# A decoder trunk on one Trainium2 core: the softmax probabilities of all four heads are multiplied by one over their sum on ScalarE, none on VectorE

## The chip, the core and the metric

The kernel runs on one core of a Trainium2 chip. The core has a matrix engine (TensorE, PE in the profile, with its weight loads as PEld), a vector engine (VectorE, DVE), a scalar engine (ScalarE, ACT), a general engine (GpSimd, POOL) and a queue that issues transfers (SyncE, SP). Each engine takes its instructions in the order in which they were written, and they meet through counting semaphores: an instruction adds one when it is done, and others wait for a count. The metric is the time of one execution on the device in microseconds, the median of several runs.

## The reference, cut to what matters

Two layers of a decoder on 1024 tokens with 1024 channels in float32. Layer 0 mixes with a retention, layer 1 with a sliding-window attention; behind each comes an MLP with a squared ReLU. The change lies in the attention of layer 1:

```
scores = q k^T * dh**-0.5            # 128 queries against 256 keys: the block before and its own
scores = where(mask, scores, -inf)
probs  = softmax([scores, sink])     # the sink, one number per head, only adds to the sum
o      = probs[..., :-1] v
```

There are 16 query heads in 4 groups that share a key and a value head each, so a group has 4 query heads. The 1024 tokens are 8 blocks of 128 queries. One block of one group is therefore a matrix of 128 queries (the partitions) by 4 heads by 256 keys, each head of which is to be divided by its own sum in each row.

## The kernel before, in words

Products of float32 are made as three products of a high and a low part: ACT rounds an operand to its high part, DVE subtracts to get the low part, and PE runs hi x hi, hi x lo and lo x hi (`product`, L480 to L482). Layer 0 comes first, the attention of layer 1 runs from about 1565 to 2000 us, and the MLP of layer 1 follows.

The attention is a pipeline over 32 items, i = 8 g + t, for group g of 0 to 3 and block t of 0 to 7. The function `sw_steps` writes, for each engine, one step s at a time, and in a step the parts of several items side by side. Group 0 is written out, groups 1 and 2 are a hardware loop of two turns, group 3 is written out and has two steps more, in which the pipeline drains and the next stage begins. In step s the engines do, in this order:

- PE: `a_pe`, the projection of block s to queries, keys and values (24 matmuls); `b_pe`, the transposes of queries and keys of block s-1 (L1797 to L1799); `d_pe`, the eight transposes of the probabilities of block s-2 (L1816), which wait for the semaphore sw_prob; half of `f_pe`, the output projection of earlier blocks; `c_pe`, the scores of block s-1; the other half of `f_pe`; `e_pe`, probabilities times values of block s-2.
- ACT: `sq_act`, squares for the norm of block s (L1856); `qkT_act`, qT_hi and kT_hi of block s-1 (L1881, L1882); `copy_act` (L1863, L1866); `pT_act`, the high part of the transposed probabilities of block s-2; now and then a split of weights; `exp_act`, four exponentials of block s-1, each with its row sum (L1897); `oT_act` (L1907); `prob_act`, the multiply of block s-1 by rden (L1873).
- DVE: `qkT_dve`, qT_lo and kT_lo of block s-1 (L1914, L1915); then the low part of v, the norm, the low part of the transposed probabilities, the mask and the maximum of block s-1, woven together; sometimes weight splits; the adds of the output projection into xT (L652); `oT_dve` (L2035); `den_dve`, the sum with the sink and its reciprocal rden (L1963); `prob_dve`, the multiply of block s-1 (L2029).
- POOL: the rotary embedding of block s (L2005 to L2023).

The probabilities lie in one buffer, prob, which the profile names xn, since it is the memory of the tile xn. It holds the masked scores, then the exponentials, then the probabilities, all in place. `prob_act` multiplies heads 2 and 3 in two instructions with one scale per row each, and only the second adds to sw_prob; `prob_dve` multiplies heads 0 and 1 in one instruction and adds one. Two increments an item are what `d_pe` waits for. Both multiplies wait for rden, through the semaphore sw_den. `den_dve` also waits until the item before has been multiplied, since rden is overwritten.

Of the kernel before, what the change touches and what calls it, by code (L numbers as in the profile page):

```python
# [25 lines left out]
ALU = mybir.AluOpType  # L26
ACT = mybir.ActivationFunctionType
AX = mybir.AxisListType

P = 128  # L30
# [3 lines left out]
TT = S // P  # L34
# [86 lines left out]
def wait(eng, sem, value):  # L121

    if isinstance(value, int) and value <= 0:
        return
    eng.wait_ge(sem, value)


def trunk(nc, x_in, positions, norm_mix, norm_mlp, w_up, w_down, ret_in, ret_out, sw_in, q_gain,
          k_gain, sinks, sw_out, c_ident, c_causal, c_mask, c_head, c_freq, c_freq_row, out, y_dram, x_dram, a_dram, r_dram):
    ctx = ExitStack()  # L130
    with ctx:
# [276 lines left out]
        sw_den = sem("sw_den")  # L408
# [1400 lines left out]

        def d_pe(pe, g, t):  # L1810
            i = TT * g + t
            pe.wait_ge(sw_prob, 2 * (i + 1))
            for s in range(2):
                wait(pe, sw_plo, 2 * (i - 1) + s + 1)
                for hh in range(4):
                    last = pe.transpose(ps[:, SP_ + s, hh * P:(hh + 1) * P], prob[:, hh, s, :], ident[:])  # L1816
                last.then_inc(d_mm, 1)
# [51 lines left out]
        def prob_act(act, g, t):  # L1869
            i = TT * g + t  # L1870
            act.wait_ge(sw_den, 2 * (i + 1))
            for hh in (2, 3):
                last = act.activation(prob[:, hh, :, :], prob[:, hh, :, :], ACT.Copy, scale=rden[:, hh:hh + 1])  # L1873
            last.then_inc(sw_prob, 1)

        def qkT_act(act, g, t):
            i = TT * g + t
# [79 lines left out]
        def den_dve(dve, g, t):  # L1957
            i = TT * g + t
            dve.wait_ge(sw_exp, 5 * (i + 1))
            wait(dve, sw_prob, 2 * i)  # L1960
            dve.tensor_tensor(den[:], ssum[:], esink[:], ALU.add).then_inc(sw_den, 1)
            dve.wait_ge(sw_den, 2 * i + 1)
            dve.reciprocal(rden[:], den[:]).then_inc(sw_den, 1)  # L1963
# [33 lines left out]
        def rope_sw_pool(pool, g, t):  # L1997
# [23 lines left out]
            pool.tensor_tensor(q4[:, :, 1, :], q4[:, :, 1, :], s4[:, 0:nq, 0, :], ALU.add)  # L2021
            pool.tensor_tensor(k3[:, 0, :], k3[:, 0, :], s4[:, nq, 1, :], ALU.subtract)
            pool.tensor_tensor(k3[:, 1, :], k3[:, 1, :], s4[:, nq, 0, :], ALU.add).then_inc(sw_radd, 1)  # L2023

        def prob_dve(dve, g, t):
            i = TT * g + t
            dve.wait_ge(sw_den, 2 * (i + 1))
            half = prob[:, 0:2, :, :].rearrange("p h s n -> p h (s n)")
            dve.tensor_tensor(half, half, rden[:, 0:2].unsqueeze(2).to_broadcast([P, 2, 2 * P]),  # L2029
                               ALU.mult).then_inc(sw_prob, 1)  # L2030

        def oT_dve(dve, g, t):
            i = TT * g + t
# [78 lines left out]
        def sw_steps(which, eng):  # L2112
# [9 lines left out]
            def run(f, g, s, lag):  # L2122
                it = item(g, s, lag)
                if it and (s - lag < TT):
                    f(eng, *it)

            def step(g, s, last_group):
# [49 lines left out]
                if which == "dve":  # L2177
                    run(qkT_dve, g, s, 1)
                    run(vlo_dve, g, s, 0)
                    run(var_dve, g, s, 0)  # L2180
                    behind = item(g, s, 2)
                    lows = [lambda j=j: pT_dve(eng, *behind, j) for j in range(2)] if behind and s - 2 < TT else []
                    softmax = item(g, s, 1)
                    masks = ([lambda j=j: mask_half(eng, *softmax, j) for j in range(2)] +
                             [lambda j=j: max_dve(eng, *softmax, j) for j in range(2)] +
                             [lambda j=j: sink_dve(eng, *softmax, j) for j in range(2)]
                             if softmax and s - 1 < TT else [])
                    if s == TT - 1 and not last_group:
                        splits = [lambda j=j: sw_split_lo(eng, g + 1, j) for j in range(4)]
                        work = lows + splits[:2] + masks[:2] + splits[2:] + masks[2:]  # L2190
                    else:
                        work = lows + masks
                    if s < TT:
                        scale_dve(eng, g, s, work)
                    else:
                        for w in work:
                            w()
                    if s in (4, 6):
                        for j in range(s, s + 2):
                            sw_split_lo(eng, g, j)  # L2200
                    behind_out = item(g, s, FLAG)
                    if last_group and s >= FLAG:
                        for m in range(4 * (s - FLAG), min(4 * (s - FLAG) + 4, KT)):
                            add(eng, DG_SW + g, m, BDS)
                        between_dve(eng, s)
                    elif behind_out:
                        for c in range(2):
                            add(eng, DG_SW + behind_out[0], 2 * behind_out[1] + c, BDS)
                    run(oT_dve, g, s, 2)
                    run(den_dve, g, s, 1)  # L2210
                    run(prob_dve, g, s, 1)
                    if begins and s == 0:
                        for m in range(KT, TILES):
                            norm_low(eng, m)
                    if begins and s == 1:
                        norm_rstd(eng, 2, 1)
                    if last_group:
                        drain_dve(eng, s)
# [332 lines left out]
```

## Time and profile before

| | us |
|---|---|
| median of 3 runs | 2682.6 |
| lowest and highest | 2678.55, 2683.26 |
| the profiled execution, whole | 2680.5 |
| its span in the profile | 2678.9 |

| engine | busy us | share of the span |
|---|---|---|
| PE | 2578.7 | 96% |
| PEld | 2153.6 | 80% |
| DVE | 1795.0 | 67% |
| ACT | 931.0 | 35% |
| POOL | 289.1 | 11% |

The times of the trace are microseconds from the start of the span. "Busy" is the time in which an engine executes; waiting is not in it. A line of the timeline gives the start, the time taken, the engine, the line of the kernel, the operation with its output and inputs, and how many instructions stand in the row; in brackets stands how long the engine had been idle before it, and which instruction ended that. Instructions of one engine overlap at their ends, so their distance from start to start is shorter than the time of one. "issue" is idle time for which the profile shows no wait.

### The profile page before, as it was taken

Reading aid. Unit: us, or ns where it says so; the run is one execution under the profiler, and the core shown is the slowest. Engines: PE = TensorE matmul, PEld = TensorE weight load, DVE = VectorE, ACT = ScalarE, POOL = GpSimd, SP = SyncE. Lnnn points to the kernel's source line nnn. Section 1 sums busy time; section 2 is a strip of 40 time slices with the busy share of each in tenths; the row PEclk is TensorE's granted clock in tenths of the full one; section 3 lists DMA queues with packets and bytes.
Section 4 is the critical chain, followed back from the end, with each engine's and each line's share of the span. In section 5 each row is a group of like instructions: output and inputs, shape, how many; then the busy total and the mean of one; then the engine's idle time right before and its main releaser. Section 6 shows DMA issues by size and latency. Waiting matters only on the chain.

```text
span 2678.9 us, 36897 instructions
## 1 busy us (share of the span) xinstructions
PE 2578.7 (96%) x11929; PEld 2153.6 (80%) x11929; DVE 1795.0 (67%) x3397; ACT 931.0 (35%) x1732; POOL 289.1 (11%) x344
## 2 busy tenths in 40 slices
PE   8999999999999999999999988999888999999999
PEld 6878878878788888888888877888767888888887
DVE  7545444454576876667677788888867666676775
ACT  6232332323311544442121255555554444311111
POOL 2102011020000300000000043322320000000000
PEclk9999999999999999999999999999989999999999
DMA  6012110121333333254222201001013323522222
GB/s 207 24 52 67 52 61 23 48 72 32 134 108 96 111 134 123 88 176 131 100 94 95 87 21 40 17 24 40 18 69 119 116 96 110 204 96 101 94 94 86
DMA packets 161735, 231.77 MB, mean 87 GB/s; under 512 B 21681, under 2 KB 103889, under 8 KB 161618
## 3 DMA queue, kind: packets, MB, share of 16 engines
q1 hardware_dynamic: 159314, 226.10, 25.8%
q10 hardware_dynamic: 2304, 4.20, 0.4%
q8 instruction: 63, 1.03, 0.2%
q14 instruction: 54, 0.44, 0.1%
HBM read 171.53 MB, written 58.73 MB: 86 GB/s over the span
## 4 chain that ended last, share of the span: by engine, by line
PE 81%; DVE 10%; issue 5%; ACT 3%; DMA 0%; POOL 0%; DVEq 0%; ACTq 0%; SPq 0%
PE ps L480 26%; PE ps L482 26%; PE ps L481 26%; ACT xn L1897 1%; DVE xT L652 1%; DVE wqg_lo L449 1%; PE ps L1292 1%; PE ps L1293 1%; DVE hT_lo L527 1%; PE ps L1294 1%; DVE smax L1944 1%; DVE pT_lo L1921 1%; DVE hss L1977 1%; PE ps L1340 0%; PE ps L1324 0%
## 5 line engine op out<-in xcount | busy, mean ns | idle before, releaser
L652 DVE TENSOR_TENSOR xT<-ps,xT 128x512 f32<-128x512 f32 x704 | 482.2, 689 | 268.1 <-PE ps L482 267.9
L480 PE MATMUL ps<-aT_hi,wd_hi 128*128 128x512 f32 x1408 | 554.9, 394 | 12.1 <-DVE xT L652 9.8
L481 PE MATMUL ps<-aT_lo,wd_hi 128*128 128x512 f32 x1408 | 550.4, 391 | 0.0
L482 PE MATMUL ps<-aT_hi,wd_lo 128*128 128x512 f32 x1408 | 550.4, 391 | 0.0
L480 PE MATMUL ps<-bh,uw_hi 128*128 128x512 f32 x880 | 343.8, 391 | 9.5 <-DVE uw_lo L740 8.6
L482 PE MATMUL ps<-bh,uw_lo 128*128 128x512 f32 x880 | 343.4, 390 | 0.0
L481 PE MATMUL ps<-bl,uw_hi 128*128 128x512 f32 x880 | 343.3, 390 | 0.0
L480 PEld LDWEIGHTS ps<-aT_hi,wd_hi 128*128 128x128 f32 x1408 | 265.9, 189 | 68.7 <-issue 13.2
L482 PEld LDWEIGHTS ps<-aT_hi,wd_lo 128*128 128x128 f32 x1408 | 265.7, 189 | 55.5
L481 PEld LDWEIGHTS ps<-aT_lo,wd_hi 128*128 128x128 f32 x1408 | 266.1, 189 | 54.2
L442 ACT ACTIVATE aT_hi<-raw 128x1024 fp32r<-128x1024 f32 x80 | 80.5, 1051 | 596.7 <-PE ps L482 583.1
L480 PEld LDWEIGHTS ps<-bh,uw_hi 128*128 128x128 f32 x880 | 165.7, 188 | 44.8 <-DVE uw_lo L740 9.2
L482 PEld LDWEIGHTS ps<-bh,uw_lo 128*128 128x128 f32 x880 | 165.8, 188 | 34.8
L481 PEld LDWEIGHTS ps<-bl,uw_hi 128*128 128x128 f32 x880 | 165.8, 188 | 34.0
L1557 DVE BATCH_NORM_STATS2 bn<-ps 128x6 f32<-128x512 f32 x32 | 22.4, 699 | 157.0 <-PE ps L482 157.0
L1897 ACT ACTIVATE xn<-xn,nmax 128x256 f32<-128x256 f32 x128 | 63.6, 498 | 145.3 <-DVE sdif L1955 145.3
L758 DVE TENSOR_TENSOR uw_lo<-raw,uw_hi 128x512 fp32r<-128x512 f32 x112 | 76.9, 690 | 53.2 <-ACT uw_hi L753 52.4
L758 DVE TENSOR_TENSOR uw_lo<-us,uw_hi 128x512 fp32r<-128x512 f32 x84 | 58.0, 692 | 74.6 <-ACT uw_hi L753 74.6
L480 PE MATMUL ps<-wqg_hi,hT_hi 128*128 128x512 f32 x256 | 100.1, 391 | 4.9 <-DVE wqg_lo L449 4.9
L480 PE MATMUL ps<-wv_hi,hT_hi 128*128 128x512 f32 x256 | 102.1, 399 | 0.0
L480 PE MATMUL ps<-ws_hi,hT_hi 128*128 128x384 f32 x256 | 89.0, 348 | 11.7 <-DVE ws_lo L1769 6.7
L482 PE MATMUL ps<-wv_hi,hT_lo 128*128 128x512 f32 x256 | 99.8, 390 | 0.0
(285 smaller groups left out, 4706.3 us busy)
## 6 DMA issues: line engine op xcount, KB each, us to landing
raw<-in_w_up SPq DMA_DIRECT2D x64, 512.0 KB, 5.5
raw<-in_w_down SPq DMA_DIRECT2D x64, 512.0 KB, 3.4
raw<-a_dram SPq DMA_DIRECT2D x64, 512.0 KB, 3.3
raw<-in_ret_w_in SPq DMA_DIRECT2D x48, 512.0 KB, 4.9
a_dram<-upost SPq DMA_DIRECT2D x64, 256.0 KB, 2.1
a_dram<-xn SPq DMA_DIRECT2D x64, 256.0 KB, 2.0
xT<-x_dram SPq DMA_DIRECT2D x24, 512.0 KB, 6.3
y_dram<-xn SPq DMA_DIRECT2D x32, 256.0 KB, 2.3
```

The source lines that it names most:

```text
L442: act.activation(dst, src, ACT.Copy).then_inc(w_hi, 1)
L449: dve.tensor_tensor(dst, src, hi.bitcast(F32), ALU.subtract).then_inc(w_lo, 1)
L480: pe.matmul(bank, ah, bh, start=(begin and i == 0), stop=False, skip_group_check=not begin)
L481: pe.matmul(bank, ah, bl, start=False, stop=False, skip_group_check=not begin)
L482: last = pe.matmul(bank, al, bh, start=False, stop=(i == len(pairs) - 1), skip_group_check=not begin)
L527: dve.scalar_tensor_tensor(hT_lo[:, k, cols], xT[:, k, cols], gain(2, k), hT_hi[:, k, cols].bitcast(F32), ALU.mult, ALU.subtract).then_inc ...
L652: dve.tensor_tensor(xT[:, k, cols], ps[:, banks[m % len(banks)], :], xT[:, k, cols], ALU.add).then_inc(x_add, 1)
L758: dve.tensor_tensor(uw(uw_lo, s % URING), weight(i, q), uw(uw_hi, s % URING).bitcast(F32), ALU.subtract).then_inc(u_lo, 1)
L1292: pe.matmul(bank, wh, hT_hi[:, k, cols], start=(k == 0), stop=False)
L1293: pe.matmul(bank, wh, hT_lo[:, k, cols], start=False, stop=False)
L1294: last = pe.matmul(bank, wl, hT_hi[:, k, cols], start=False, stop=(k == KT - 1))
L1897: act.activation(prob[:, hh, :, :], prob[:, hh, :, :], ACT.Exp, bias=nmax[:, hh:hh + 1], accum_out=ssum[:, hh:hh + 1]).then_inc(sw_exp, 1)
```

## The change

All four heads are multiplied by ACT, each in an instruction of 128 x 256 elements with its own increment of sw_prob. DVE's multiply of 128 x 512 elements is gone. The count that `d_pe` and `den_dve` wait for is four an item instead of two. Nothing else is moved, and no transfer is touched.

```diff
--- before.py
+++ after.py
@@ -1809,7 +1809,7 @@
 
         def d_pe(pe, g, t):
             i = TT * g + t
-            pe.wait_ge(sw_prob, 2 * (i + 1))
+            pe.wait_ge(sw_prob, 4 * (i + 1))
             for s in range(2):
                 wait(pe, sw_plo, 2 * (i - 1) + s + 1)
                 for hh in range(4):
@@ -1869,9 +1869,9 @@
         def prob_act(act, g, t):
             i = TT * g + t
             act.wait_ge(sw_den, 2 * (i + 1))
-            for hh in (2, 3):
-                last = act.activation(prob[:, hh, :, :], prob[:, hh, :, :], ACT.Copy, scale=rden[:, hh:hh + 1])
-            last.then_inc(sw_prob, 1)
+            for hh in range(4):
+                act.activation(prob[:, hh, :, :], prob[:, hh, :, :], ACT.Copy,
+                               scale=rden[:, hh:hh + 1]).then_inc(sw_prob, 1)
 
         def qkT_act(act, g, t):
             i = TT * g + t
@@ -1957,7 +1957,7 @@
         def den_dve(dve, g, t):
             i = TT * g + t
             dve.wait_ge(sw_exp, 5 * (i + 1))
-            wait(dve, sw_prob, 2 * i)
+            wait(dve, sw_prob, 4 * i)
             dve.tensor_tensor(den[:], ssum[:], esink[:], ALU.add).then_inc(sw_den, 1)
             dve.wait_ge(sw_den, 2 * i + 1)
             dve.reciprocal(rden[:], den[:]).then_inc(sw_den, 1)
@@ -2021,13 +2021,6 @@
             pool.tensor_tensor(q4[:, :, 1, :], q4[:, :, 1, :], s4[:, 0:nq, 0, :], ALU.add)
             pool.tensor_tensor(k3[:, 0, :], k3[:, 0, :], s4[:, nq, 1, :], ALU.subtract)
             pool.tensor_tensor(k3[:, 1, :], k3[:, 1, :], s4[:, nq, 0, :], ALU.add).then_inc(sw_radd, 1)
-
-        def prob_dve(dve, g, t):
-            i = TT * g + t
-            dve.wait_ge(sw_den, 2 * (i + 1))
-            half = prob[:, 0:2, :, :].rearrange("p h s n -> p h (s n)")
-            dve.tensor_tensor(half, half, rden[:, 0:2].unsqueeze(2).to_broadcast([P, 2, 2 * P]),
-                               ALU.mult).then_inc(sw_prob, 1)
 
         def oT_dve(dve, g, t):
             i = TT * g + t
@@ -2208,7 +2201,6 @@
                             add(eng, DG_SW + behind_out[0], 2 * behind_out[1] + c, BDS)
                     run(oT_dve, g, s, 2)
                     run(den_dve, g, s, 1)
-                    run(prob_dve, g, s, 1)
                     if begins and s == 0:
                         for m in range(KT, TILES):
                             norm_low(eng, m)
```

## Rows read from the trace of the kernel before

**Rows 1.** The page of the profile, first part.
```profile
PE 2578.7 (96%) x11929; PEld 2153.6 (80%) x11929; DVE 1795.0 (67%) x3397; ACT 931.0 (35%) x1732; POOL 289.1 (11%) x344
```

**Rows 2.** Busy time by stretch: engines, granted clock, DMA share, GB/s.
```profile
1662.00:1761.00 99.00, 93.47 (x537) 83.88 (x536) 85.73 (x256) 53.07 (x164) 29.63 (x56) 0.98 0.10 28
1755.00:1758.00 3.00, 3.00 (x11) 3.00 (x11) 2.83 (x12) 2.44 (x10) 1.33 (x3) 0.50 0.41 144
```

**Rows 3.** Waits, 1585 to 1985 us: total us, times, longest.
```profile
DVE qT_lo L1914 <- ACT kT_hi L1882: 37.4, 29, 3.4
ACT xn L1873 <- DVE rden L1963: 35.6, 32, 2.4
PE ps L1797 <- DVE xT L652: 4.3, 6, 1.0
```

**Rows 4.** Timeline, DVE: start us, us taken, line, operation, idle before it.
```profile
1719.47 0.18 DVE L1963 RECIPROCAL rden<-den 128x4 f32<-128x4 f32 x1
1730.83 0.18 DVE L1963 RECIPROCAL rden<-den 128x4 f32<-128x4 f32 x1
1731.04 0.69 DVE L2029 TENSOR_TENSOR xn<-xn,rden 128x512 f32<-128x512 f32 x1
1732.94 0.42 DVE L1914 TENSOR_TENSOR qT_lo<-ps,qT_hi 128x256 fp32r<-128x256 f32 x1 [1.21 <-ACT kT_hi L1882]
```

**Rows 5.** Timeline, ACT, the same step.
```profile
1731.04 0.91 ACT L1873 ACTIVATE xn<-xn,rden 128x256 f32<-128x256 f32 x2 [0.77 <-DVE rden L1963]
1731.86 0.51 ACT L1856 ACTIVATE scr<-ps,rstd 128x320 f32<-128x320 f32 x1
1732.27 0.37 ACT L1881 ACTIVATE qT_hi<-ps 128x256 fp32r<-128x256 f32 x1
1732.53 0.38 ACT L1882 ACTIVATE kT_hi<-ps 128x256 fp32r<-128x256 f32 x1
```

**Rows 6.** Timeline, PE, the step before it and the same step.
```profile
1718.14 0.34 PE L482 MATMUL ps<-ws_hi,hT_lo 128*128 128x384 f32 x1
1720.64 1.09 PE L1816 MATMUL ps<-ident,xn 128*128 128x128 f32 x8 [0.88 <-ACT xn L1873]
1731.68 0.27 PE L1799 MATMUL ps<-ident,kr 128*128 128x128 f32 x1
1732.01 1.09 PE L1816 MATMUL ps<-ident,xn 128*128 128x128 f32 x8
```

**Rows 7.** Groups by line, 1585 to 1985 us: busy us, mean ns, idle before.
```profile
L1873 ACT ACTIVATE xn<-xn,rden 128x256 f32<-128x256 f32 x64 | 29.1, 501 | 35.6 <-DVE rden L1963 35.6
L2029 DVE TENSOR_TENSOR xn<-xn,rden 128x512 f32<-128x512 f32 x32 | 22.3, 697 | 1.1
```

**Rows 8.** Timeline, ACT, DVE and PE: the steps unlike the others.
```profile
1587.66 0.38 ACT L1881 ACTIVATE qT_hi<-ps 128x256 fp32r<-128x256 f32 x1 [0.97 <-PE ps L1799]
...
1622.69 0.38 ACT L1881 ACTIVATE qT_hi<-ps 128x256 fp32r<-128x256 f32 x1 [0.44 <-PE ps L1799]
...
1762.37 0.42 DVE L1914 TENSOR_TENSOR qT_lo<-ps,qT_hi 128x256 fp32r<-128x256 f32 x1 [2.54 <-issue]
...
1930.73 0.53 ACT L1856 ACTIVATE scr<-ps,rstd 128x320 f32<-128x320 f32 x1 [0.33 <-PE ps L482]
...
1952.39 0.53 ACT L1856 ACTIVATE scr<-ps,rstd 128x320 f32<-128x320 f32 x1 [2.10 <-PE ps L482]
...
1968.17 1.09 PE L1816 MATMUL ps<-ident,xn 128*128 128x128 f32 x8 [1.72 <-ACT xn L1873]
```

**Rows 9.** Timeline, POOL, a step of the first group and the same step as above.
```profile
1620.97 0.77 POOL L2022 TENSOR_TENSOR kr<-kr,scr 128x32 f32<-128x32 f32 x1
...
1730.71 0.25 POOL L2022 TENSOR_TENSOR kr<-kr,scr 128x32 f32<-128x32 f32 x1
```

**Rows 10.** Timeline, PE, behind the weights' split.
```profile
1753.84 0.44 PE L480 MATMUL ps<-ws_hi,hT_hi 128*128 128x384 f32 x1 [2.23 <-DVE ws_lo L1769]
...
1755.05 0.53 PE L480 MATMUL ps<-ws_hi,hT_hi 128*128 128x384 f32 x1
```

## The prediction

> **What bounds the kernel now.** I read four views in turn. The page's first part [rows 1] says TensorE (PE) is busy 96% of the span, VectorE (DVE) 67%, ScalarE (ACT) 35%. An average does not tell who waits for whom, so I cut out the attention stage, 1585 to 1985 us, where every multiply by rden lies. In one group of eight blocks, 1662 to 1761 us, PE is busy 93.5 of 99 us, DVE 85.7 and ACT 53.1 [rows 2]. DVE looks full and ACT half empty. The third view, who waited for whom, is where that picture breaks [rows 3]: DVE's qT_lo (L1914), the first DVE instruction of each step, waited 29 times for ACT's kT_hi (L1882), 37.4 us in all, and ACT's multiply (L1873) waited for DVE's rden all 32 times. The two engines hand the work to each other, and neither overlaps the hand-over.
>
> The timeline of one step shows the loop [rows 4, 5]. DVE writes rden at 1730.83 and both engines start at 1731.04. DVE multiplies heads 0 and 1 in 0.69 us, then stands idle 1.21 us. ACT multiplies heads 2 and 3 (two passes in one row, 0.91 us with the tail of the second), then in its own order the square of the next block (1731.86), qT_hi (1732.27) and kT_hi (1732.53, ending 1732.91). Only then can DVE start qT_lo, at 1732.94. From there DVE works through its list to rden, with a hand to ACT for the exponentials on the way. One turn is the distance between two rden: 1730.83 - 1719.47 = 11.36 us [rows 4]. So the multiply on ACT is in series with the turn, and the multiply on DVE is not: it lies beside ACT's and ends 1.21 us before anyone wants DVE.
>
> PE has little room of its own, but is not what sets the turn. Its transposes of the probabilities (L1816) start at 1732.01, directly behind the end of ACT's second multiply (1731.04 + 0.91 = 1731.95), and 0.33 us after the start of a transpose that takes 0.27 [rows 5, 6]: PE had come to them slightly before ACT was done. In the steps with more DVE work PE waits for it openly, 0.88 us at 1720.64 [rows 6].
>
> **The change part by part.** *Removed:* 32 DVE multiplies, 22.3 us of DVE time [rows 7]. Worth: nothing where the 1.21 us gap follows, as the gap only grows from 1.21 to 1.90 us. *Added:* two more 128x256 multiplies a block on ACT. What one adds to ACT's queue is not its 0.501 us but its start-to-start time: the square behind the two starts 1731.86 - 1731.04 = 0.82 us after the first, so 0.41 each and 0.82 for two [rows 5]. If the two more did not overlap they would cost 2 x 0.501 = 1.00; if the first of a batch were the dear one, 2 x 0.26 = 0.52, from the nearest cheaper pass: kT_hi, 256 columns from PSUM without a scale, starts 0.26 after qT_hi (1732.27 to 1732.53). I take 0.82, since it is the same instruction at the same place. The three more semaphore increments a block I cost at nothing, as qT_hi and kT_hi each carry one and start 0.26 apart. PE's and DVE's waits change only their number: PE still waits for the last head. Queued behind the longer ACT batch are square, qT_hi, kT_hi, qk_raw and the splits of the transposed probabilities; waiting for it are PE (d_pe, and all that is behind it in order) and DVE's qT_lo. Both are shifted by the same 0.82, so nothing that DVE needs later from PE comes later in relation to it.
>
> **How many steps pay.** There are 32 multiplies. The full 0.82 is paid where ACT's own queue releases the next step. Of the 29 waits of qT_lo for kT_hi, four are not of that kind [rows 8]: in the first block qT_hi waited 0.97 us for PE, which covers the 0.82, cost 0; at 1622.69 it waited 0.44 us, which leaves 0.82 - 0.44 = 0.38; at 1930.73 ACT's square waited 0.33 for PE, leaving about 0.4; at 1952.39 it waited 2.10, cost 0. That leaves 25. The last block but one has no such wait, but PE waits 1.72 us for the multiply there [rows 8]: the 26th. In the last block PE has other work until after the multiply: 0. The turn of the hardware loop, at 1762.37, is a case of its own: DVE came 2.54 us after the end of its multiply, held by "issue" and not by ACT, which elsewhere is ready 1.21 us after that end [rows 4, 8]. Without its multiply DVE would be ready 2.54 - 0.69 = 1.85 after the same point, and ACT 1.21 + 0.82 = 2.03 after it: 0.5 earlier than the 2.54 of now. The bounds are -0.5 and +0.82 (if the turn of the loop waits on something else that moves), and I take -0.5.
>
> Sum: 26 x 0.82 = 21.3; plus 0.4, plus 0.4, minus 0.5: **+21.6 us**. By the bounds of two passes (0.52 and 1.00) it is +13.8 to +26.3. There is no DMA in the change, and none of the waits above is for one. The profiled execution took 2680.5 us, so it would take 2702.1; it is 2.1 us below the median of the three runs, 2682.6, from which the sum gives 2704.2. I put the forecast between, nearer the median: **2703.5 us**.
>
> A small thing in the trace: at 1620.97 POOL's subtraction L2022 takes 0.77 us while DVE's multiply runs, and 0.25 at 1730.71, before DVE's multiply begins [rows 9]. The Trainium skill (SBUF — State Buffer, Who interferes with whom) says that a DVE instruction with two SBUF inputs contends with a GpSimd instruction that reads SBUF; this row agrees. By that rule the removed multiply gives POOL back about 0.5 us there, and also in the first block. It would take at most 0.1 us off my sum, since with POOL earlier ACT's queue is the later of the two.
>
> **Rivals.**
> *DVE's relief wins (faster).* If the turn were set by DVE's own queue, each of the same 26 steps would lose 0.69 us: 26 x 0.69 = 18 us, 2682.6 - 18 = 2665. For it speaks 85.7 of 99 us busy against ACT's 53.1 [rows 2]. It decides from the point where DVE's idle time after its multiply is zero; the rows show 1.21 us [rows 4], and a wait at 29 of 32 places [rows 3]. Chance 2%. The Trainium skill (Perfetto Trace Analysis, Optimizing Scalar/DVE Operations) says that where DVE is saturated, offloading some work to Scalar may make sense; that is this rival, and the waits speak against it here.
> *The extra ACT time is covered (no change).* If PE set the turn and had other work before d_pe, ACT's 0.82 would fit into slack: about 2683 to 2688. For it: PE is busy 93.5 of 99 us. Against it: PE takes its work in order, and its wait for ACT at L1816 shows already (0.88 us) [rows 6]. Chance 5%, and another 5% that half the steps are covered, about 2694.
> *The clock falls more often (slower still).* After PE waited 2.23 us for DVE's ws_lo at 1753.84, the granted clock was 0.50, 1.2 GHz, from 1755 to 1758 us; a matmul of the projection that takes 0.34 us elsewhere took 0.53 [rows 2, 6, 10]. Three microseconds at half clock are 1.5 us of PE's work lost. In the steps where PE waits both for DVE's xT (6 times, 4.3 / 6 = 0.7 us) and for ACT's multiply (0.88), it will wait 0.7 + 0.88 + 0.82 = 2.4 us in two pieces [rows 3, 6]. Six such falls, none covered, are 6 x 1.5 = 9 us: 2712. Against it: in those steps PE's projection is done early (1718.14 + 0.34 = 1718.48, while rden, behind which ACT's multiply and square still come, is only at 1719.47), so most of a fall would be hidden [rows 4, 6]. Chance 8%. The Trainium skill (TensorE: Matmul & The Clock Gate, HAM oscillation) says that gaps in PE's work bring the slow clock back at the next start; one gap of 2.2 us here agrees.
> *The change does nothing of what it says:* I see no way; the counts of the waits fit the four increments.
>
> **How the numbers follow.** The forecast has 80%, the clock rival 8%, half cover 5%, no change 5%, faster 2%. The range goes from 2695, just below two passes at 0.52 us (2682.6 + 13.8 = 2696), to 2712, which takes in passes of 0.50 us and the clock rival. About 0.2%, 5.4 us, is what a measurement of this kernel can tell from no change. Faster 0.02, same 0.05, slower 0.93.
>
> **What would show it.** In steady steps: L1873 in four passes, the last starting 1.23 us after the first; the square 1.64 us after the first; rden to rden 12.18 us; DVE idle 2.7 us before qT_lo (1.21 + 0.69 + 0.82); PE's wait before L1816 about 1 us in every step instead of 0.2. The stage 1585 to 1985 grows by 21 to 22 us, and nothing outside it changes. I would be wrong if passes cost less than 0.41 in a row of four, if DVE takes up work in the gap, or if the slow clock shows in steps where it did not before.

## The result and the profile after

| | kernel before | changed kernel |
|---|---|---|
| median, us | 2681.6 (4 runs, 2678.55 to 2683.26) | 2706.6 (4 runs, 2703.86 to 2708.9) |
| ratio | | 1.0094 [1.0077, 1.0112] |
| profiled execution, us | 2680.5 | 2708.9 |
| its span, us | 2678.9 | 2707.3 |

The changed kernel is 0.94% slower, 25.0 us by the medians and 28.4 us by the two profiled executions. The forecast was 2703.5 us, the range 2695 to 2712. All times here and below are of executions at the usual granted clock; a fifth execution of the kernel with PE filled, at a clock of 0.65, took 3731.8 us and is left out.

The busy line of the page, answering [rows 1]: VectorE has lost its 22 us and ScalarE has gained 25, while TensorE's share is unchanged. Nothing in this line says that 25 us were lost.

```profile
PE 2585.8 (96%) x11929; PEld 2158.0 (80%) x11929; DVE 1772.9 (65%) x3365; ACT 955.9 (35%) x1796; POOL 287.9 (11%) x344
```

Who waited for whom in the attention, 1585 to 2010 us (us in all, times, longest), answering [rows 3]. DVE's wait for kT_hi has gone from 37.4 us to 82.4. PE's wait for xT (L1797, 4.5 us) is about the 4.3 us of before. A wait of PE for the multiply now stands behind nearly every block, 28.6 / 28 = 1.0 us each.

```profile
DVE qT_lo L1914 <- ACT kT_hi L1882: 82.4, 30, 4.2
ACT xn L1873 <- DVE rden L1963: 35.5, 31, 2.7
...
PE ps L1816 <- ACT xn L1873: 28.6, 28, 2.5
...
PE ps L1797 <- DVE xT L652: 4.5, 6, 1.0
```

The step of [rows 4 to 6] in the changed kernel, from the timelines of DVE, ACT and PE:

```profile
1728.04 0.18 DVE L1963 RECIPROCAL rden<-den 128x4 f32<-128x4 f32 x1
...
1740.19 0.18 DVE L1963 RECIPROCAL rden<-den 128x4 f32<-128x4 f32 x1
...
1743.10 0.42 DVE L1914 TENSOR_TENSOR qT_lo<-ps,qT_hi 128x256 fp32r<-128x256 f32 x1 [2.72 <-ACT kT_hi L1882]
```
```profile
1740.41 1.71 ACT L1873 ACTIVATE xn<-xn,rden 128x256 f32<-128x256 f32 x4 [0.77 <-DVE rden L1963]
1742.02 0.51 ACT L1856 ACTIVATE scr<-ps,rstd 128x320 f32<-128x320 f32 x1
...
1742.69 0.37 ACT L1882 ACTIVATE kT_hi<-ps 128x256 fp32r<-128x256 f32 x1
```
```profile
1742.17 1.09 PE L1816 MATMUL ps<-ident,xn 128*128 128x128 f32 x8 [0.84 <-ACT xn L1873]
```

The square starts 1742.02 - 1740.41 = 1.61 us after the first multiply, where it was 0.82 [rows 5]: 0.79 for two more passes. DVE stands idle 2.72 us, and one turn, rden to rden, is 1740.19 - 1728.04 = 12.15 us, where it was 11.36 [rows 4]. The distance between two rden is the yardstick of all that follows. I call turn k the one that ends with the rden of item k (i = 8 g + t), so turn 15 holds the turn of the hardware loop and turn 30 lies in the drain. The shift at item k is how much later its rden comes than in the kernel before, counted in both from the first rden.

Set against the kernel before, turn by turn, with both profiled executions:

| turns | forecast, us | measured, us |
|---|---|---|
| 26 that pay in full | 26 x 0.82 = 21.3 | 26 x 0.79 = 20.5 |
| extra in 16 and 20, over the 0.79 | 0 | +0.84 and +0.87 |
| extra in 13, 21 and 27, over the 0.79 | 0 | +0.33, +0.31 and -0.35 |
| 1 | 0 | -0.30 |
| 4 | +0.4 | +0.23 |
| 15, the turn of the loop | -0.5 | +1.93 |
| 29 | +0.4 | +0.31 |
| 30 | 0 | +1.60 |
| sum over the attention | +21.6 | +26.2 |

The rest of the 28.4 us lies outside: 1.6 us are there when the attention's first rden is written (1586.74 for 1585.16), and 0.6 come behind the last. The 1.6 is no effect of the change. Of the kernels below, all alike up to that point, the first rden falls between 1580.8 and 1586.1 us, and a good part of that spread is TensorE's clock before it. The stretch from 713 to 724 us, in layer 0, in the kernel before and in the same kernel with its hardware loop written out (length; busy us of PE, PEld, DVE, ACT, POOL; granted clock; share of the DMA queues; GB/s):

```profile
713.00:724.00 11.00, 8.75 (x24) 6.36 (x23) 8.55 (x20) 3.69 (x5) 1.28 (x1) 0.54 1.00 391
```
```profile
713.00:724.00 11.00, 9.22 (x38) 7.00 (x37) 9.55 (x22) 3.71 (x5) 1.30 (x1) 0.84 1.02 392
```

The first is granted 0.54 of full clock and does 24 matmuls, the second 0.84 and does 38. Of the profiled executions, the five with 0.84 or more there write the first rden between 1580.8 and 1582.4 us, the seven with 0.61 or less between 1584.6 and 1586.7. So whole times carry some 4 us that belong to neither kernel. (The two profiled executions of this result both have the low clock there, 0.54 and 0.61; where their 1.6 us arose is open.) From here on I give, beside each median, the time from the first rden to the end of the span: 1093.7 us before, 1120.6 after, +26.8. It is read from one execution of each kernel; the repetition below shows how far it holds.

### The profile page after: what moved, and what is told of

It reads as the page before. It is cut to its first block, busy times and chain, and to the rows that moved or that the text cites. A ratio compares the mean times of both kernels' runs of the same rounds, so it can differ in the third digit from the quotient of the medians.

```text
span 2707.3 us, 36943 instructions
## 1 busy us (share of the span) xinstructions
PE 2585.8 (96%) x11929; PEld 2158.0 (80%) x11929; DVE 1772.9 (65%) x3365; ACT 955.9 (35%) x1796; POOL 287.9 (11%) x344
## 4 chain that ended last, share of the span: by engine, by line
PE 81%; DVE 10%; issue 5%; ACT 4%; DVEq 0%; DMA 0%; ACTq 0%
PE ps L480 26%; PE ps L482 26%; PE ps L481 26%; ACT xn L1897 1%; ACT xn L1873 1%; DVE xT L652 1%; DVE wqg_lo L449 1%; PE ps L1292 1%; DVE hT_lo L527 1%; PE ps L1294 1%; PE ps L1293 1%; DVE smax L1944 1%; DVE pT_lo L1921 0%; PE ps L1340 0%; DVE hss L1977 0%
## 5 line engine op out<-in xcount | busy, mean ns | idle before, releaser
L480 PE MATMUL ps<-aT_hi,wd_hi 128*128 128x512 f32 x1408 | 557.5, 396 | 12.1 <-DVE xT L652 9.8
L480 PE MATMUL ps<-bh,uw_hi 128*128 128x512 f32 x880 | 343.8, 391 | 9.5 <-DVE uw_lo L740 8.6
L480 PEld LDWEIGHTS ps<-aT_hi,wd_hi 128*128 128x128 f32 x1408 | 267.2, 190 | 68.9 <-issue 13.2
L480 PEld LDWEIGHTS ps<-bh,uw_hi 128*128 128x128 f32 x880 | 165.8, 188 | 44.8 <-DVE uw_lo L740 9.2
L1557 DVE BATCH_NORM_STATS2 bn<-ps 128x6 f32<-128x512 f32 x32 | 22.4, 699 | 157.0 <-PE ps L482 157.0
L480 PE MATMUL ps<-wqg_hi,hT_hi 128*128 128x512 f32 x256 | 100.1, 391 | 4.9 <-DVE wqg_lo L449 4.9
L480 PE MATMUL ps<-wv_hi,hT_hi 128*128 128x512 f32 x256 | 102.1, 399 | 0.0
L449 DVE TENSOR_TENSOR aT_lo<-raw,aT_hi 128x1024 fp32r<-128x1024 f32 x80 | 97.3, 1218 | 3.9 <-ACT aT_hi L442 3.9
```

The costliest lines, as they stand in the source:

```text
L449: dve.tensor_tensor(dst, src, hi.bitcast(F32), ALU.subtract).then_inc(w_lo, 1)
L480: pe.matmul(bank, ah, bh, start=(begin and i == 0), stop=False, skip_group_check=not begin)
```

## The experiments

The theory: DVE and ACT hand each block to each other, ACT's multiply lies in that loop and DVE's does not, so the time goes up by what ACT's queue takes longer, and what DVE gives up is worth nothing. The rivals: DVE's relief counts, PE covers part of it, or TensorE's clock carries the loss.

**ACT's part alone.** ACT multiplies heads 2 and 3 once more into memory that nothing reads, in 30 of 32 blocks, ahead of the two multiplies in place. DVE keeps its own.

```diff
+        def i_early(g, t):
+            return not (isinstance(g, int) and g == SW_KV - 1 and t >= TT - 2)
+
         def prob_act(act, g, t):
             i = TT * g + t
             act.wait_ge(sw_den, 2 * (i + 1))
+            for hh in (2, 3) if i_early(g, t) else ():
+                act.activation(xn[:, 1, (hh - 2) * 2 * P:(hh - 1) * 2 * P].rearrange("p (s n) -> p s n", n=P),
+                               prob[:, hh, :, :], ACT.Copy, scale=rden[:, hh:hh + 1])
             for hh in (2, 3):
...
```

> The kernel before with two more multiplies on ACT: each block, ACT first multiplies heads 2 and 3 into a spare buffer (30 of the 32 blocks) and then in place, while DVE keeps its own multiply. So it is the addition alone. Queue theory (ACT's multiply is in series with the turn, DVE's lies beside it): a steady turn goes from 11.36 to 12.15 us as in the changed kernel, and the time is that of the changed kernel less about 1 us for the two blocks left out, +23 to +26 us on before. If DVE's multiply were part of what set the turn, keeping it would cost up to 0.69 x 26 = 18 us more than the changed kernel.

Measured: 2702.8 us, ratio 1.0080 [1.0063, 1.0097], +25.0 us from the first rden on. (By the medians it is 20.9 us, below the 23 to 26 expected; this profiled execution has the early first rden, 1580.8 us.) DVE in one step, its lines six further down than in the other kernels:

```profile
1722.48 0.18 DVE L1969 RECIPROCAL rden<-den 128x4 f32<-128x4 f32 x1
...
1734.63 0.18 DVE L1969 RECIPROCAL rden<-den 128x4 f32<-128x4 f32 x1
...
1734.85 0.69 DVE L2035 TENSOR_TENSOR xn<-xn,rden 128x512 f32<-128x512 f32 x1
...
1737.54 0.42 DVE L1920 TENSOR_TENSOR qT_lo<-ps,qT_hi 128x256 fp32r<-128x256 f32 x1 [2.00 <-ACT kT_hi L1888]
```

The turn is 12.15 us with the multiply still on DVE, to the hundredth that of the changed kernel. The loss in the steady turn is ACT's two passes. DVE has 2.00 us left over where it had 1.21, so whether it multiplies or not can't be seen in the turn.

**DVE's part alone.** DVE's multiply is taken out of the kernel before, and ACT does its two heads as ever. Heads 0 and 1 stay undivided by their sums, which is left out of the computation here.

```diff
-            pe.wait_ge(sw_prob, 2 * (i + 1))
+            pe.wait_ge(sw_prob, i + 1)
...
-            wait(dve, sw_prob, 2 * i)
+            wait(dve, sw_prob, i)
...
-                    run(prob_dve, g, s, 1)
```

> The kernel before without DVE's multiply: heads 0 and 1 stay unnormalised, ACT multiplies heads 2 and 3 as before. So it is the removal alone. Queue theory: no change within 0.1% apart from the turn of the hardware loop, where DVE came late (gain up to 1.3 us); the steady turn stays 11.36 us and DVE's idle time before qT_lo goes from 1.21 to 1.90 us. Relief theory (DVE's own queue sets the turn): 18 us faster, turn 10.67 us.

Measured: 2679.6 us, ratio 0.9991 [0.9982, 1.0001], -0.7 us from the first rden on.

```profile
1719.39 0.18 DVE L1963 RECIPROCAL rden<-den 128x4 f32<-128x4 f32 x1
...
1730.74 0.18 DVE L1963 RECIPROCAL rden<-den 128x4 f32<-128x4 f32 x1
...
1732.86 0.43 DVE L1914 TENSOR_TENSOR qT_lo<-ps,qT_hi 128x256 fp32r<-128x256 f32 x1 [1.93 <-ACT kT_hi L1882]
```

22 us of VectorE's work are gone and the turn is still 11.35 us; the idle time has grown from 1.21 to 1.93. The rival that DVE's relief would win is out. Small amounts do appear in single turns: -0.44 and -0.52 in turns 1 and 4, -0.41 in turn 15, +0.33 and +0.31 in turns 13 and 21, -2.2 over turns 27 to 29, +1.58 in turn 30. The last two go with TensorE's clock: over turns 28, 29 and 30 it was granted 0.86, 0.83 and 1.00 in the kernel before and 1.00, 0.91 and 0.91 here. The two halves of the change sum to 25.0 - 0.7 = 24.3 us, for 26.8 of the whole. In the steady turns they add up; in single turns they do not. Turn 31 has no added passes in the first half (0.8 us), turn 30 has its 1.6 us in either half and only once in the whole, and the 2.2 us that this half wins in turns 27 to 29 are mostly not won in the whole.

**Three heads on ACT, one on DVE.** One more pass instead of two, in the kernel before.

```diff
-            for hh in (2, 3):
+            for hh in range(1, 4):
...
+            half = prob[:, 0:1, :, :].rearrange("p h s n -> p h (s n)")
...
```

> Half of the change: ACT multiplies heads 1, 2 and 3, DVE head 0. Queue theory, linear: the steady turn is 11.36 + 0.40 = 11.76 us, and the time half of the change, +11 to +13 us. Clock theory (a part of the loss comes with a threshold, when PE's waits grow long enough for the clock to fall in more places): less than half, about +10, with no half-speed stretch that before does not have.

Measured: 2692.9 us, ratio 1.0033 [1.0023, 1.0044], +12.9 us from the first rden on.

```profile
1723.57 0.18 DVE L1963 RECIPROCAL rden<-den 128x4 f32<-128x4 f32 x1
...
1735.33 0.18 DVE L1963 RECIPROCAL rden<-den 128x4 f32<-128x4 f32 x1
```
```profile
1735.54 1.31 ACT L1873 ACTIVATE xn<-xn,rden 128x256 f32<-128x256 f32 x3 [0.77 <-DVE rden L1963]
```

The turn is 11.76 us: 11.36, 11.76, 12.15 for two, three and four passes, 0.40 each, on a straight line. The Trainium skill (ScalarE: Activation LUTs, What ACT_TABLE_LOAD costs) gives an ACTIVATE 186 ns + 0.833 ns an element, 93 ns more for a pointer operand, and an overlap of 93 ns back to back; worked out from these figures, an estimate, 256 elements with a scale of one number per row take 0.49 us alone and 0.40 from start to start. The rows agree with both: the last of four passes lasts 1.71 - 3 x 0.40 = 0.51 us in the changed kernel, and each adds 0.40 to a turn.

**The changed kernel once more**, unaltered, to see what repeats.

> The changed kernel once more, for what differs between executions. Queue theory: steady turns 12.15 us again, ACT held again at the turn of the hardware loop (1.2 us before its square, 1.0 us before qk_raw), time within 0.2% of 2706.6. Clock theory: the two extra half-speed stretches (1787.5 and 1838.6 us in the first profile, 0.85 us each in the turn around them) lie elsewhere, or are absent, in this profile, and the time moves with their number.

Measured: 2707.0 us, ratio 1.0082 [1.0065, 1.0099], +27.2 us from the first rden on. The extra time is in turns 16 and 20 again, to 0.02 us. Two turns do not repeat so well: turn 15 costs +1.66 us instead of +1.93, and turn 30 +2.32 instead of +1.60, at a granted clock of 0.83 instead of 0.91. ACT is held behind the turn of the loop again:

```profile
1772.40 0.53 ACT L1856 ACTIVATE scr<-ps,rstd 128x320 f32<-128x320 f32 x1 [1.04 <-issue]
```

**The hardware loop written out.** The two middle groups become Python's loop, in the kernel before and in the changed one. Nothing else changes.

```diff
-            with eng.Fori(1, SW_KV - 1) as g:
+            for g in range(1, SW_KV - 1):
                 group(g, False)
```

> The kernel before with the hardware loop over groups 1 and 2 written out in the program, nothing else changed. Loop-turn theory (the 2.54 us by issue at 1762.37 are DVE fetching the loop's first instructions anew): DVE's wait there becomes 1.21 us like the others, 1.3 us faster in that turn. Rival (instructions come late wherever the program goes): straight code shows holds by issue of its own, no gain.

> The changed kernel with the same loop written out. Loop-turn theory: ACT is no longer held (1.2 us before its square and 1.0 us before qk_raw), so turn 15 costs 0.79 us on before like the others, and the distance to the kernel before without the loop is the sum of the steady turns and the clock, 23 to 25 us. Also, if the two extra half-speed stretches (turns 16 and 20) hang on where the steps fall against the clock's rhythm rather than on PE's waits alone, the shift of 2 us at the loop moves or removes them.

Measured: the kernel before without the loop takes 2678.5 us, ratio 0.9990 [0.9981, 0.9999], and the changed one without it 2700.9 us, ratio 1.0072 [1.0056, 1.0087]; from the first rden on they are at -3.5 and +23.7 us. To see what the loop does, first DVE in the changed kernel with it, at turn 15, then ACT there:

```profile
1770.18 0.18 DVE L1963 RECIPROCAL rden<-den 128x4 f32<-128x4 f32 x1
...
1774.41 0.42 DVE L1914 TENSOR_TENSOR qT_lo<-ps,qT_hi 128x256 fp32r<-128x256 f32 x1 [4.05 <-ACT kT_hi L1882]
```
```profile
1770.39 1.70 ACT L1873 ACTIVATE xn<-xn,rden 128x256 f32<-128x256 f32 x4 [1.14 <-DVE rden L1963]
...
1773.30 0.53 ACT L1856 ACTIVATE scr<-ps,rstd 128x320 f32<-128x320 f32 x1 [1.21 <-issue]
...
1775.38 0.53 ACT L1863 ACTIVATE qk_raw<-ps,rstd 128x320 f32<-128x320 f32 x1 [1.00 <-issue]
```

and ACT in the changed kernel without the loop, at the same place:

```profile
1765.29 1.70 ACT L1873 ACTIVATE xn<-xn,rden 128x256 f32<-128x256 f32 x4 [1.15 <-DVE rden L1963]
1766.90 0.51 ACT L1856 ACTIVATE scr<-ps,rstd 128x320 f32<-128x320 f32 x1
...
1767.83 0.53 ACT L1863 ACTIVATE qk_raw<-ps,rstd 128x320 f32<-128x320 f32 x1
```

With the loop, ACT waits for nothing that the profile shows, 1.21 us before the square and 1.00 us before qk_raw; without it both waits are gone. The turn goes from 12.84 us to 11.34 in the kernel before and from 14.77 to 12.13 in the changed one. So the turn of the loop costs 1.5 us in the one and 2.6 in the other, and without a loop the change costs 12.13 - 11.34 = 0.79 there as in a steady turn. In the kernel before it was DVE that was held [rows 8], and ACT was not. The whole cost of the change hardly falls without the loop: 2700.9 - 2678.5 = 22.4 us by the medians, but 23.7 + 3.5 = 27.1 from the first rden on, where 23 to 25 were expected. What turn 15 no longer costs is back in turns 29 and 30, which cost 1.5 and 2.7 us; the clock in turn 30 is 0.83 for 1.00.

**PE kept at work while it waits.** Six transposes of the identity, whose results nothing reads, ahead of PE's wait for the multiply in every block of the changed kernel.

```diff
         def d_pe(pe, g, t):
             i = TT * g + t
+            wait(pe, sw_plo, 2 * (i - 1) + 1)
+            for _ in range(6):
+                pe.transpose(ps[:, SP_, 0:P], ident[:], ident[:])
             pe.wait_ge(sw_prob, 4 * (i + 1))
```

> The changed kernel with six throwaway transposes of the identity (0.11 us each, 0.65 us) on PE before it waits for the probabilities, into the bank that the real transposes overwrite. They fit into PE's wait of 0.8 to 0.9 us. Clock theory (the longer wait of PE is what brings the extra half-speed stretches): the stretches in turns 16 and 20 (+1.65 instead of +0.79) vanish, the steady turn stays 12.15 us, and the time falls by 1.5 to 3 us against the changed kernel. Rival (the stretches come from PE's earlier waits in the step, or from its columns as a whole): they stay where they are, and the time stays, or rises where PE has no wait to fill.

It answers what turns 16 and 20 showed. In the changed kernel and in the kernel before, the windows of these two turns (columns as above; the turns are 13.1 and 13.0 us after, 11.5 and 11.4 before), and, of the changed kernel, a stretch inside the first in which PE is busy without a gap:

```profile
1785.00:1798.00 13.00, 11.73 (x60) 10.58 (x61) 9.14 (x30) 6.69 (x21) 3.37 (x8) 0.87 0.00 0
1787.50:1790.70 3.20, 3.20 (x12) 2.78 (x11) 2.78 (x9) 1.92 (x6) 0.87 (x1) 0.53 0.00 0
1836.10:1849.10 13.00, 11.33 (x58) 10.13 (x57) 9.16 (x30) 6.69 (x21) 3.10 (x6) 0.87 0.24 66
```
```profile
1771.80:1783.20 11.40, 10.93 (x65) 9.96 (x65) 9.76 (x31) 5.91 (x19) 3.44 (x8) 1.00 0.00 0
1819.00:1830.30 11.30, 10.43 (x63) 9.46 (x62) 9.71 (x31) 5.90 (x19) 3.15 (x6) 1.00 0.26 72
```

The granted clock is 0.53 from 1787.5 to 1790.7, TensorE's lower level, 1.2 GHz, and full in the same turns of before. With PE filled, the same two turns:

```profile
1782.00:1794.30 12.30, 11.57 (x70) 10.61 (x71) 9.15 (x31) 6.69 (x21) 3.53 (x8) 1.00 0.00 0
1832.40:1844.50 12.10, 11.09 (x69) 10.14 (x67) 9.04 (x30) 6.70 (x21) 3.08 (x6) 1.00 0.27 72
```

The clock is full, and both turns are back at +0.79. The shift at item 28 is 21.5 us instead of 23.5. But the whole time is 2704.9 us, ratio 1.0085 [1.0069, 1.0100], and +26.6 us from the first rden on: turns 29 and 30, at +0.94 and +2.63 instead of +0.31 and +1.60, give back what was won (the granted clock of turn 30 is 0.83, as in the repetition of the changed kernel). So the idle time of PE costs 1.7 us in turns 16 and 20 by way of the clock, and removing it does not shorten the stage. By the medians the kernel is about 2 us shorter than the changed one, which is less than the executions of either scatter.

**The other direction: all four heads on DVE, or three.** If ACT's passes are what counts, taking them away from ACT should win.

```diff
...
-            half = prob[:, 0:2, :, :].rearrange("p h s n -> p h (s n)")
+            full = prob[:, 0:4, :, :].rearrange("p h s n -> p h (s n)")
...
-                    run(prob_act, g, s, 1)
```

> The change turned round: DVE multiplies all four heads in one instruction of 128 x 1024, ACT none. Queue theory: ACT's part of the turn falls by 0.82 us and DVE's multiply, about 1.22 us, now ends behind ACT's kT_hi, so qT_lo starts 1.4 us after rden instead of 2.1. Where DVE and ACT set the turn (group 0 and the steps with weight splits, about 14) that is 0.7 us each, 10 us; in the steady turns PE, which stood only about 0.2 us in 11.36, becomes the bound at about 11.15, so 0.2 each, 2 to 3 us. Total -9 to -14 us on before. Relief theory (DVE was the bound): DVE's work grows by 0.53 us a block, 14 us slower.

Measured: 2677.4 us, ratio 0.9983 [0.9974, 0.9993], -2.7 us from the first rden on. ACT, PE and DVE in one step:

```profile
1782.19 0.53 ACT L1856 ACTIVATE scr<-ps,rstd 128x320 f32<-128x320 f32 x1 [1.46 <-PE ps L482]
```
```profile
1782.80 1.09 PE L1816 MATMUL ps<-ident,xn 128*128 128x128 f32 x8 [0.21 <-DVE xn L2029]
```
```profile
1781.30 0.18 DVE L1963 RECIPROCAL rden<-den 128x4 f32<-128x4 f32 x1
1781.51 1.24 DVE L2029 TENSOR_TENSOR xn<-xn,rden 128x1024 f32<-128x1024 f32 x1
...
1792.65 0.18 DVE L1963 RECIPROCAL rden<-den 128x4 f32<-128x4 f32 x1
```

The turn is 1792.65 - 1781.30 = 11.35 us, what it was; over the stage the steady turns lie between 10.9 and 11.7 us. I had expected 9 to 14 us less and missed: ACT's queue is free and now stands still 1.46 us for PE's projection, and PE waits 0.21 us for DVE's longer multiply. By these rows the next bound lies close behind ACT's queue: PE's projection, on which the square waits, and DVE's multiply, on which PE waits. The straight line of two, three and four passes does not go on below two.

With three heads on DVE (0.96 us) and one pass on ACT:

```diff
-            for hh in (2, 3):
+            for hh in range(3, 4):
...
-            half = prob[:, 0:2, :, :].rearrange("p h s n -> p h (s n)")
+            half = prob[:, 0:3, :, :].rearrange("p h s n -> p h (s n)")
...
```

> DVE multiplies heads 0 to 2 (128 x 768, about 0.96 us), ACT head 3. Queue theory: qT_lo starts 1.7 us after rden (-0.4); steady turns 11.15 us (PE-bound), the others -0.4: -7 to -9 us on before. Relief theory: 7 us slower.

Measured: 2678.1 us, ratio 0.9989 [0.9980, 0.9999], -2.3 us from the first rden on; 7 to 9 us less had been expected. The steady turns of the two middle groups are 10.97 to 11.43 us and the shift at item 28 is -3.9, of which turn 30, at a clock of 0.83, gives back 2.4.

**Three heads on DVE and no hardware loop.** Both edits that won a little, together.

> The best of the shifts together: DVE multiplies three heads, ACT one, and the loop over groups 1 and 2 is written out. If the two gains add (e6 0.11%, e7 0.10%), 0.2% below before, about 2675.5. If both draw on the same thing (PE, which bounds the steady turns and gives gains back in the last steps through the slow clock), 0.1%.

Measured: 2672.0 us, ratio 0.9963 [0.9950, 0.9977], -5.8 us from the first rden on. By the medians it is 10.5 us below the kernel before, where 2675.5 us was expected, and it is the only version whose interval lies more than 0.2% below. Its turns and, in the windows, one group and the drain:

```profile
1691.06 0.18 DVE L1963 RECIPROCAL rden<-den 128x4 f32<-128x4 f32 x1
1691.27 0.97 DVE L2029 TENSOR_TENSOR xn<-xn,rden 128x768 f32<-128x768 f32 x1
...
1702.34 0.18 DVE L1963 RECIPROCAL rden<-den 128x4 f32<-128x4 f32 x1
```
```profile
1656.00:1753.00 97.00, 92.07 (x540) 83.77 (x538) 88.12 (x258) 50.25 (x154) 29.98 (x58) 1.00 0.10 28
1938.90:1959.20 20.30, 15.94 (x77) 13.48 (x75) 11.38 (x34) 5.76 (x18) 3.48 (x7) 0.83 0.14 52
```

A turn is 11.28 us here, and PE is busy 92 of 97 us, so this arrangement should have little more to give. In the drain the clock is 0.83, and turn 30 costs 2.5 us more than in the kernel before.

**The multiply later in ACT's order.** If only the place in ACT's queue matters, the multiply of the changed kernel can stand behind qT_hi and kT_hi of the next step, which then are early for DVE.

```diff
                     run(qkT_act, g, s, 1)
+                    run(prob_act, g, s, 2)
...
-                    run(prob_act, g, s, 1)
```

> The changed kernel with ACT's four multiplies moved behind qT_hi and kT_hi of the next step, so that DVE's qT_lo no longer waits for them but PE's transposes do, 1.1 us longer. Queue theory: qT_lo starts 1.3 us after rden instead of 2.9, but the transposes 3.0 instead of 2.0, and behind them in PE's order stand the scores, which DVE's mask needs: the wait moves from qT_lo to the mask, and the steady turn is 12.2 to 12.5 us, no gain on the changed kernel. If only DVE's own wait at qT_lo counted, the turn would fall to 10.6 to 11.2 us, and the kernel would be faster than before by some 5 us.

Measured: 2740.7 us, ratio 1.0221 [1.0205, 1.0236], +58.5 us from the first rden on, the longest of all. PE at one step, then ACT and DVE at it:

```profile
1756.96 1.09 PE L1816 MATMUL ps<-ident,xn 128*128 128x128 f32 x8 [2.41 <-ACT xn L1873]
```
```profile
1754.15 0.53 ACT L1856 ACTIVATE scr<-ps,rstd 128x320 f32<-128x320 f32 x1 [1.97 <-PE ps L482]
1755.22 1.70 ACT L1873 ACTIVATE xn<-xn,rden 128x256 f32<-128x256 f32 x4
```
```profile
1757.64 0.28 DVE L1970 SCALAR_TENSOR_TENSOR vp_lo<-ps,rstd,vp_hi 128x64 fp32r<-128x64 f32 x1 [1.53 <-ACT vp_hi L1866]
...
1761.54 0.69 DVE L1935 SCALAR_TENSOR_TENSOR xn<-ps,swmask 128x512 f32<-128x512 f32 x1 [1.47 <-PE ps L482]
```

I had expected turns of 12.2 to 12.5 us and most of the steady ones are 13.5 to 13.7. In step after step PE waits some 2.4 us for the multiply, so what stands behind it ends later, the projection of the next block with it; ACT's square waits 1.97 us for that, and the multiply, now behind the square, is late again; DVE pays 1.53 and 1.47 us at the two places shown. The multiply has two customers, DVE by way of kT_hi and PE directly, and an order that serves the first makes the second the bound.

## Why the prediction was right, and where its steps were not

**The loop of the two engines: right, and shown.** ACT's part alone reproduces the turn of 12.15 us, DVE's part alone leaves it at 11.35. The forecast for the steady step (square 1.64 us after the first multiply, turn 12.18, DVE idle 2.7, PE about 1 us before L1816) came out as 1.61, 12.15, 2.72 and 28.6 / 28 = 1.0.

**The price of a pass: right to 0.02 us.** 0.395 a pass for 0.41, which over 26 turns is -0.8 us. The bounds of 0.26 and 0.50 were not needed. By its own words the prediction would be wrong "if passes cost less than 0.41 in a row of four"; they do, by 4%, and that sign was drawn too tight to tell anything.

**The turn of the hardware loop: wrong, by 2.4 us.** The step that failed is "ACT 1.21 + 0.82 = 2.03 after it". DVE's own lateness no longer shows, since DVE now waits for ACT, 4.05 us. (With DVE's multiply alone taken out, qT_lo starts 3.04 us after rden instead of 3.45, and still 0.96 us after the end of kT_hi: the lateness shrinks by 0.41 us, not by the 0.69 that I took.) But I took ACT's queue to pass the end of the loop unhindered because it had done so before. There ACT's queue passed without a gap between multiply and square; with the two passes more, ACT stands 1.21 us in "issue" behind them, and 1.00 us before qk_raw. The measured +1.93 lies outside my bounds of -0.5 and +0.82. That it is the loop, and not something else at this place, the two kernels without it show (1.5 us in the one, 2.6 in the other). Why the hold goes from DVE to ACT is not settled: with the loop standing, ACT is held in every kernel here in which it has more than two passes ahead of the square (1.02 us with ACT's extra passes alone, 1.71 with three passes, 1.26 with PE filled), and not in the one in which the four passes stand behind kT_hi. With one pass or none it is DVE again, 2.06 and 1.79 us. I can say when each is held, not by what.

**The clock rival: not the main thing, but part of it.** It had six falls of 1.5 us, none covered, 9 us in all. There were two new ones in the steady turns, 0.84 and 0.87 us, 1.7 us together, in turns 16 and 20, and the same in the repetition and with ACT's part alone. Just before the first, PE had waited 0.98 us for POOL and 0.73 for the multiply; around the second, 0.64 us for xT and 1.67 for the multiply, which is the wait of 2.4 us in two pieces that the rival described. With three passes there were no such falls. They are tied to PE's waiting: filled with work, PE keeps its full clock in these turns. The sum had no added fall, and this term was 1.7 us too low; with the fall in turn 30, told next, it was 3.3. The slow clock in steps where it was not before is also one of the signs by which the prediction said that it would be wrong. The Trainium skill (TensorE: Matmul & The Clock Gate, HAM oscillation) says that gaps in PE's work bring the slow clock back at the next start; it gives the sign, which the rows of turns 16 and 20 bear out, and not the number of falls, which had to be counted.

**Turn 30: wrong, by 1.6 us.** I put "2.10, cost 0" there, since the wait for PE covered ACT's 0.82. It covered it, but another fall of the clock moved in:

```profile
1974.60:1994.00 19.40, 15.05 (x77) 12.90 (x75) 10.43 (x32) 6.95 (x21) 3.49 (x7) 0.91 0.15 56
```
```profile
1949.20:1967.00 17.80, 13.44 (x77) 11.61 (x75) 11.10 (x33) 6.15 (x19) 3.50 (x7) 1.00 0.16 60
```

The first is the changed kernel, the second the one before, with the same 77 matmuls, busy 15.05 us at a clock of 0.91 for 13.44 at 1.00: 1.6 us. In both PE stands still for 3.8 us until DVE has written xT. Behind that pause the kernel before keeps its full clock, with matmuls of 0.39 us. In the changed kernel the clock falls some 1.4 us behind the pause, and from 1989 to 1991 us it is 0.50:

```profile
1961.59 0.47 PE L480 MATMUL ps<-aT_hi,wd_hi 128*128 128x512 f32 x1 [3.81 <-DVE xT L652]
```
```profile
1987.05 0.47 PE L480 MATMUL ps<-aT_hi,wd_hi 128*128 128x512 f32 x1 [3.82 <-DVE xT L652]
...
1988.91 0.63 PE L481 MATMUL ps<-aT_lo,wd_hi 128*128 128x512 f32 x1
```

In the repetition it has fallen already in the pause. It is no price of ACT's passes, as turn 30 grows by 1.6 us with DVE's multiply merely left out, and by 1.6 with all four heads on DVE as well. Every kernel in which the multiplies were touched, in either direction, has this, about 1.6 us or more; the kernel before with the loop written out has not (turn 30 as long as before, to the hundredth). The pause is equally long in both, so it alone does not settle the matter; what sets the fall off, and why the kernel before escapes it, is open.

**Small turns.** The first block came out at -0.30 us, and turn 4 at +0.23 for +0.4. In the first block it is DVE's relief: the turn loses 0.44 us with DVE's part out alone, and nothing (+0.01) with ACT's part alone. POOL's L2021 takes 0.45 us there instead of 0.90, and PE's L1797 waits for POOL; that this is the way was half foreseen and priced at "at most 0.1". In turn 4 it is not the relief, though POOL's L2022 does take 0.24 us at 1623.83 instead of 0.77 [rows 9]: with ACT's part alone L2022 still takes 0.77 us, and the turn is +0.24 all the same. ACT's queue alone makes it 12.13 to 12.14 us long, like a steady turn, so in the kernel before PE's wait stood for some 0.55 us beyond ACT's queue (11.90 - 11.35) and not for 0.44. The +0.33 in turns 13 and 21, the same place in the two turns of the hardware loop, comes with DVE's part out and not with ACT's part alone (+0.80 there, no more than elsewhere), and is gone from the changed kernel when the loop is written out (+0.77). So it needs both the missing multiply and the loop; by what way, is open. The -0.35 of turn 27 is there with DVE's part out as well (-0.34) and not with ACT's part alone.

**The range and the chances.** 2703.5 was 3.1 us below the median measured, while the stage, in the profiled executions, grew by 26.2 us for 21.6, 4.6 more. The medians show less of it, 25.0 us between them; that is luck and no merit of the forecast, and is within the 4 us that whole times carry. The differences are -0.8 (passes), +2.4 (loop), +1.6 (turn 30), +1.7 (clock in 16 and 20), +0.3 (13, 21, 27) and -0.6 (1, 4 and 29). The misses at 15, 13 and 21, and 1 are of one kind: a place where the step is not like the others, read from one execution and carried over.

## What to carry to other kernels

Before work is moved from a busy engine to one that is half idle, follow one item round the loop: here DVE was busy 86 of 99 us and ACT 53, and moving DVE's 22 us to ACT cost 25, because ACT's part lay in series and DVE's beside it. An instruction is worth its start-to-start time in the queue that releases the next step, and nothing in the other; and when it is taken out of that queue, what is late next (here, by the rows, PE, below some 11.3 us a turn) caps the gain. The Trainium skill (Perfetto Trace Analysis, Optimizing Scalar/DVE Operations) says that with a saturated DVE offloading to Scalar may make sense; the waits, not the busy shares, tell whether it does, and here they and the runs speak against it.

## What the hardware showed that I had not expected

- The end of this hardware loop holds the engines unequally. In the kernel before it holds DVE (2.54 us where 1.21 is usual, [rows 8]) and not ACT; with two passes more on ACT it holds ACT, 1.21 and 1.00 us in one kernel, 1.04 and 0.89 in its repetition. Writing the two turns out saves 1.5 and 2.6 us in that turn.
- A low clock can belong to the kernel: it came at turns 16 and 20 in both executions of the changed kernel and with ACT's part alone. Without the loop the falls lie elsewhere (turns 12 and 20). It can also differ between executions of one kernel: turn 30 of the changed kernel was granted 0.91 in one and 0.83 in the other, 19.43 and 20.15 us.
- A pause of PE does not always bring the low clock: the same 3.8 us before L480 in turn 30 are followed by full clock in the kernel before, with and without its loop, and by a fall in the changed kernel.
- What is gained early in this stage is often given back in the drain, by the clock: the 2 us in the kernel with PE filled, 2.4 of 3.9 with three heads on DVE.
- About 4 us of spread among the profiled executions, of kernels alike up to there, has its place in layer 0, where the stretch from 713 to 724 us is granted from 0.53 to 0.86.
